# Norms moved into the other stream's stages, pieces spaced by declared costs, and a second set of value buffers in the first stage of a two-layer decoder kernel

## The reference, cut to what matters

```python
# D_MODEL 1024, SEQ 2048, layer 0: retention, 4 heads (dk 256, dv 512); layer 1: window attention, 16 heads of 64
for layer in range(2):
    hp, hs = rms_norm(xp, norm_mix[layer]), rms_norm(xs, norm_mix[layer])
    if layer == 0:    # chunks of 128; the state s is carried from chunk to chunk
        yp, sp = retention_mixer(hp, pos_p, 0, 128, w_q, w_k, w_v, w_g, w_o)
        ys, ss = retention_mixer(hs, pos_s, state_ret, 8, w_q, w_k, w_v, w_g, w_o)
    else:
        yp, kp, vp = swa_prompt(hp, ...); ys, kn, vn = swa_sample(hs, cache_k, cache_v, ...)
    xp, xs = xp + yp, xs + ys
    xp = xp + swiglu(rms_norm(xp, norm_ffn[layer]), w1, w3, w2)     # (silu(x@w1) * (x@w3)) @ w2, width 2816
    xs = xs + swiglu(rms_norm(xs, norm_ffn[layer]), w1, w3, w2)
y_prompt, y_sample = rms_norm(xp, norm_final), rms_norm(xs, norm_final)
# retention, one chunk of one head: o = (q k^T * decay) v + q s ; s = s*c + (k*kdecay)^T v ;
# then per row (o - mean) * rsqrt(var + eps), times silu(h @ w_g), then @ w_o
```

## Time and profile before

| | |
|---|---|
| Median of 3 runs | 2740.5 us (2739.23 to 2741.64) |
| Profiled execution, its own time | 2740.44 us |
| Its span on the slowest core (5) | 2739.4 us; the eight cores 2719.8 to 2739.4 |
| PE (matmul) busy | 2166.1 us, 79% |
| DVE, ACT, POOL busy | 1201.0, 771.6, 145.8 us |
| Mean granted TensorE clock, core 5 | 0.882 |
| HBM read and written | 332.78 and 104.60 MB |

### The profile page before, as it was taken

One profiled execution on the slowest core, in us unless ns is written; L12 is line 12 of the kernel. 1 busy time (PEld: TensorE's weight loads), 2 busy tenths in 40 slices (PEclk: granted clock), 3 DMA queues, 4 the chain that ended last, 5 costly groups with the idle time before them and its releaser, 6 DMA issues.

```text
span 2739.4 us, 39645 instructions; the slowest of 8 cores (2719.8 to 2739.4 us)
## 1 busy us (share of the span) xinstructions
PE 2166.1 (79%) x12058; PEld 1020.5 (37%) x12058; DVE 1201.0 (44%) x3034; ACT 771.6 (28%) x1480; POOL 145.8 (5%) x273
## 2 busy tenths in 40 slices
PE   3766588878688878868888688887879887867797
PEld 2322233333233334433333233333435444433454
DVE  3454345442345434543545444554244434543423
ACT  1323122231135223412323222323023422431211
POOL 0000001001000101100000010000000000000000
PEclk9877799988789989978999889988979998988898
DMA  8563667758665669763443464532413242211233
GB/s 198 127 161 76 167 173 173 178 156 182 159 183 169 187 172 220 174 190 127 157 149 134 139 198 160 176 113 73 147 62 105 70 116 76 83 55 58 92 114 104
DMA packets 136590, 380.34 MB, mean 139 GB/s; under 512 B 19744, under 2 KB 23968, under 8 KB 136352
## 3 DMA queue, kind: packets, MB, share of 16 engines
q1 hardware_dynamic: 103024, 282.36, 32.0%
q0 software_dynamic: 33360, 95.44, 17.4%
HBM read 332.78 MB, written 104.60 MB: 160 GB/s over the span
## 4 chain that ended last, share of the span: by engine, by line
PE 56%; DVE 18%; DMA 9%; issue 8%; ACT 6%; DVEq 1%; SPq 0%; ACTq 0%; POOL 0%; POOLq 0%
PE pb L434 55%; ACT arL L443 4%; DMA wbd<-wf 3%; DVE arL L449 2%; DVE arL L461 2%; PE pb L440 2%; DVE Sst L452 2%; DVE hT L452 2%; DMA arG<-st_in 1%; DMA wf<-wt 1%; DVE stat L455 1%; DVE stat L677 1%; DMA srs<-arG 1%; DVE stat L452 1%; ACT sq L443 1%
## 5 line engine op out<-in xcount | busy, mean ns | idle before, releaser
L434 PE MATMUL pb<-hT,wf 128*128 128x512 bf16 x2816 | 700.5, 404 | 16.7 <-DVE arF L452 5.6
L434 PEld LDWEIGHTS pb<-hT,wf 128*128 128x128 bf16 x2816 | 284.0, 103 | 381.9 <-issue 113.1
L434 PE MATMUL pb<-arF,wf 128*128 128x512 bf16 x1408 | 338.6, 391 | 4.4 <-DMA wf<-wt 4.1
L443 ACT ACTIVATE arL<-pb 128x512 bf16<-128x512 f32 (+2 forms) x278 | 200.0, 728 | 261.7 <-PE pb L434 219.0
L434 PE MATMUL pb<-wl,hT 128*128 128x512 bf16 (+1 forms) x1152 | 254.7, 374 | 5.3 <-DVE Sst L452 5.3
L452 DVE SCALAR_TENSOR_TENSOR arF<-arF,pb 128x512 f32<-128x512 f32 (+1 forms) x176 | 121.1, 688 | 299.5 <-ACT arF L443 229.3
L449 DVE TENSOR_TENSOR xT<-pb,xT 128x512 f32<-128x512 f32 x160 | 108.9, 690 | 317.0 <-PE pb L434 316.9
L434 PE MATMUL pb<-hT,wl 128*128 128x512 bf16 x800 | 217.7, 413 | 29.9 <-DVE hT L452 12.6
L440 PE MATMUL pb<-cbt,arL 128*128 128x128 bf16 x1056 | 97.8, 235 | 134.2 <-DVE arL L449 86.5
L434 PEld LDWEIGHTS pb<-arF,wf 128*128 128x128 bf16 x1408 | 138.0, 101 | 168.7 <-issue 29.0
L443 ACT ACTIVATE arF<-pb 128x512 f32<-128x512 f32 x176 | 105.8, 601 | 332.4 <-PE pb L434 326.5
(11 more groups left out here) (89 smaller groups left out, 2004.3 us busy)
## 6 DMA issues: line engine op xcount, KB each, us to landing
wl<-wbd SPq DMA_DIRECT2D x123, 512.0 KB, 5.0
wf<-wbd SPq DMA_DIRECT2D x120, 512.0 KB, 4.2
wf<-wbd SPq DMA_DIRECT2D x96, 352.0 KB, 3.2
arG<-st_in SPq DMA_DIRECT2D x128, 256.0 KB, 4.1
srs<-arG POOLq DMA_DIRECT2D x128, 256.0 KB, 3.5
wl<-wt POOLq DMA_DIRECT2D x41, 512.0 KB, 7.6
wbd<-wl SPq DMA_DIRECT2D x41, 512.0 KB, 10.0
wf<-wt POOLq DMA_DIRECT2D x40, 512.0 KB, 8.8
```

The costliest lines, as they stand in the source:

```text
L434: S.op("pe", lambda e: e.matmul(out, lhsT, rhs, start=start, stop=stop), r, w)
L443: S.op("act", lambda e: e.activation(out=out, in_=in_, func=func, bias=bias, scale=scale), r, w)
```

## The change

- `run`'s stages are paired anew. The norm that feeds a tile's next mixer now stands at the end of the feed-forward part of the stage before (`nm(0, 2, PF)` and its like, `swap`), and the norm that feeds a tile's feed-forward at the start of the feed-forward part, while part 0 starts at once with matmuls on an `hT` that is ready. In stage 8 the two norms for stage 9 stand at the end of part 0. The norm of tile 1 for stage 2 runs in stage 1 (`first_x1`).
- The `pc` numbers of `norm`, `scores` and `core` are raised; `norm` of a tile now counts 4 times 1300, then 4500, 2500 and 1500.
- `ffn` yields between the w1 and the w3 matmuls of a 512-column tile, and its first activation (for tanh also the VectorE instruction behind it) is recorded before the w3 matmuls, for the sample's 128 columns too.
- `layer0` of stage 1 (`deep`) has kd, v and g twice, the second set in `arF`, and lets out all of the next head's projections between its chunks; in the last head it lets out w_o matmuls of heads 0 to 2. `wo` adds into `xT` behind each 4 matmuls of the last head instead of at the end of a half.
- `gstream` loads its states on the POOL queue instead of SP's.
- The first loads stand in another order, and `load_x(1)` comes later. `swap` loads a later tile 10000 units of `pc` ahead of its norm.

```diff
@@ norm
-                    pc(60 * nch)
                     if kc % 2 == 1:
+                        pc(1300 if NT == TT else 700)
                         yield
...
                 rsq(n_[:, 0:nch], n_[:, 4:4 + nch], n_[:, 8:8 + nch], nb)
+                pc(4500)
                 yield
...
-                pc(500 * nch)
+                pc(2500)
                 yield
...
                     if after is not None:
                         after(kc)
+                pc(1500)
                 yield
@@ ffn
                                     b1, b3 = b1_[:, 0:NS], b3_[:, NS:2 * NS]
                                 else:
                                     b1, bb1, _ = pb(P)
-                                    b3, bb3, _ = pb(P)
+                                s1v = o.s1[:, s, :NT]
                                 for kc in range(KC):
                                     mm(b1[:, :NT], w1u[:, kc, fi * 128:(fi + 1) * 128], cx.hT[:, kc, :NT], kc == 0, kc == KC - 1,
                                        [w1b_, cx.hb[kc]], [bb1])
+                                if tanh:
+                                    act(s1v, b1[:, :NT], AF.Tanh, [bb1], [o.s1b[s]], scale=0.5)
+                                    stt(s1v, s1v, 1.0, b1[:, :NT], ALU.add, ALU.mult, [o.s1b[s], bb1], [o.s1b[s]])
+                                else:
+                                    act(s1v, b1[:, :NT], AF.Silu, [bb1], [o.s1b[s]])
+                                pc(8 * NT * 0.43)
+                                if NT > NS:
+                                    yield
+                                    b3, bb3, _ = pb(P)
                                 for kc in range(KC):
                                     mm(b3[:, :NT], w3u[:, kc, fi * 128:(fi + 1) * 128], cx.hT[:, kc, :NT], kc == 0, kc == KC - 1,
                                        [w3b_, cx.hb[kc]], [bb3])
-                                pc(16 * NT * 0.43)
-                                s1v = o.s1[:, s, :NT]
+                                pc(8 * NT * 0.43)
                                 if tanh:
-                                    act(s1v, b1[:, :NT], AF.Tanh, [bb1], [o.s1b[s]], scale=0.5)
-                                    stt(s1v, s1v, 1.0, b1[:, :NT], ALU.add, ALU.mult, [o.s1b[s], bb1], [o.s1b[s]])
                                     stt(o.aT[:, fl, :NT], s1v, 0.5, b3[:, :NT], ALU.mult, ALU.mult, [o.s1b[s], bb3], [o.ab[fl]])
                                 else:
-                                    act(s1v, b1[:, :NT], AF.Silu, [bb1], [o.s1b[s]])
                                     tt(o.aT[:, fl, :NT], s1v, b3[:, :NT], ALU.mult, [o.s1b[s], bb3], [o.ab[fl]])
                             if fi == nf - 1:
                                 RF.done(2)
@@ layer0
-            def layer0(cx, tile_i, P, rider=None, sfin=None):
+            def layer0(cx, tile_i, P, rider=None, sfin=None, deep=False):
...
+                if deep:
+                    AF_.reset()
+                kdA, vvA, ggA, kdbA, vbA, gbA = [], [], [], [], [], []
+                for A in ([AL, AF_] if deep else [AL]):
+                    kdA.append(A.alloc("kd", [128, nch, 256], BF16))
+                    vvA.append(A.alloc("v", [128, nch, 512], BF16))
+                    ggA.append(A.alloc("g", [128, nch, 512], BF16))
+                    kdbA.append([A.buf("kd") for _ in range(nch)])
+                    vbA.append([A.buf("v") for _ in range(nch)])
+                    gbA.append([A.buf("g") for _ in range(nch)])
+                nset = len(kdA)
...
+                def wo(half, hs):
+                    if hs[0] == 0:
+                        wob_[half] = [pb(P, True) for _ in range(4)]
+                    bs = wob_[half]
+                    if sfin is not None and half == 0 and hs[0] == 0:
+                        SF.c, SF.uTs, SF.uTsb = sfin()
+                    for h in hs:
...
+                            if h == RH - 1:
+                                kc = half * 4 + dm
+                                tt(cx.xT[:, kc, :NT], bs[dm][0][:, :NT], cx.xT[:, kc, :NT], ALU.add, [bs[dm][1], cx.xb[kc]], [cx.xb[kc]])
+                                P.free(bs[dm][2])
...
+                    if deep and nx:
+                        pieces = [p_qk(hd + 1, 0), p_qk(hd + 1, 1), p_vg(hd + 1, "v"), p_kd(hd + 1), p_vg(hd + 1, "g")]
+                    elif deep:
+                        pieces = [wo(0, list(range(RH - 1)))]
+                    else:
+                        pieces = [p_qk(hd + 1, 0), p_qk(hd + 1, 1)] if nx else []
+                    def step(n=1):
+                        while pieces and n:
+                            try:
+                                next(pieces[0])
+                                n -= 1
+                            except StopIteration:
+                                pieces.pop(0)
+                    scores(hd, 0)
+                    step(2 if deep else 1)
+                    pc(800)
+                    yield
+                    for c in range(nch):
+                        if c + 1 < nch:
+                            scores(hd, c + 1)
+                        core(hd, c)
+                        pc(1500)
+                        yield
+                        step(2 if deep else 1)
+                        if c > 0:
+                            tail(hd, c - 1)
+                        yield
+                        if deep:
+                            step(2 if nx else 1)
+                    while pieces:
+                        step()
+                        yield
...
+                if deep:
+                    yield from wo(0, [RH - 1])
+                else:
+                    yield from wo(0, list(range(RH)))
+                yield from wo(1, list(range(RH)))
@@ gstream
-                        dma("sp", S0[n % NR][:, :], st_in[b, h][a * 128:(a + 1) * 128, :], [], [S0b[n % NR]], f"g{n % NR}")
+                        dma("pool", S0[n % NR][:, :], st_in[b, h][a * 128:(a + 1) * 128, :], [], [S0b[n % NR]], f"g{n % NR}")
@@ body
...
+            def swap(t, P):
+                load_x(t)
+                pc(10000)
+                yield
+                yield from norm(pcx[t % 2], 0, P)
...
+            dma("pool", cb[:, 0:256], cb_d[:, 0:256], (), [cbb], "c1")
+            load_x(0)
+            RL.fill(2)
+            dma("sp", cf[:, :], cf_d[:, :], (), [cfb], "c2")
             dma("sp", sp[:, :], spar[:, :], (), [spb], "c0")
-            load_x(0)
-            dma("sp", cf[:, :], cf_d[:, :], (), [cfb], "c2")
-            dma("pool", cb[:, 0:256], cb_d[:, 0:256], (), [cbb], "c1")
-            RL.fill(3)
+            load_rope(0)
             dma("pool", cb[:, 256:CB_N], cb_d[:, 256:CB_N], (), [cbb2], "c3")
-            load_rope(0)
...
-            res[1] = run(1, [(lstage0(0, P1, rider=(s0c, rope_s)), 0, 1)])
+            def first_x1():
+                load_x(1)
+                pc(100)
+                yield
+                yield from norm(pcx[1], 0, P1)
+            res[1] = run(1, [(chain(norm(pcx[0], 0, P1), norm(s0c, 0, P1), layer0(pcx[0], 0, P1, (s0c, rope_s), None, True)), 0, 1), (first_x1(), 0.3, 0.85)])
             g = gstream()
             gall.append(g)
-            res[2] = run(2, [(lstage0(1, PL), 0, 1), (fstage(0, 0, False, PF), 0, 1)], 16, g)
+            res[2] = run(2, [(layer0(pcx[1], 1, PL), 0, 1), (chain(nm(0, 1, PF), ffnp(0, 0, False, PF), nm(0, 2, PF)), 0, 0.93)], 16, g)
             dma("sp", ks_o[:, 0:128 - DS, :], ck[:, DS:128, :], [], [], "ko")
             dma("sp", vs_o[:, 0:128 - DS, :], cv[:, DS:128, :], [], [], "ko")
-            res[3] = run(3, [(lstage1(0, PL), 0, 1), (fstage(1, 0, True, PF), 0, 1)], 40, g)
-            res[4] = run(4, [(lstage1(1, PL), 0, 1), (fstage(0, 1, True, PF), 0, 0.9)], 8, g)
-            res[5] = run(5, [(lstage0(2, PL), 0.12, 1), (fstage(1, 1, False, PF), 0, 0.92)], 38, g)
-            res[6] = run(6, [(lstage0(3, PL, sf=sfin), 0.12, 1), (fstage(2, 0, False, PF), 0, 1)], 26, g, 0.55)
-            res[7] = run(7, [(lstage1(2, PL), 0, 1), (fstage(3, 0, True, PF4, True), 0, 1)])
-            res[8] = run(8, [(lstage1(3, PL, True), 0, 1), (fstage(2, 1, True, PF), 0, 1)])
-            res[9] = run(9, [(fstage(3, 1, False, P1, True), 0, 1)])
+            res[3] = run(3, [(layer1(pcx[0], 0, PL), 0, 1), (chain(nm(1, 1, PF), ffnp(1, 0, True, PF), nm(1, 2, PF)), 0, 0.93)], 40, g)
+            res[4] = run(4, [(layer1(pcx[1], 1, PL), 0, 1), (chain(nm(0, 3, PF), ffnp(0, 1, True, PF), fin(0, PF), swap(2, PF)), 0, 0.95)], 8, g)
+            res[5] = run(5, [(layer0(pcx[0], 2, PL), 0, 1), (chain(nm(1, 3, PF), ffnp(1, 1, False, PF), fin(1, PF), swap(3, PF)), 0, 0.95)], 38, g)
+            res[6] = run(6, [(layer0(pcx[1], 3, PL, None, sfin), 0, 1), (chain(nm(2, 1, PF), ffnp(2, 0, False, PF), nm(2, 2, PF)), 0, 0.93)], 26, g, 0.55)
+            res[7] = run(7, [(layer1(pcx[0], 2, PL), 0, 1), (chain(nm(3, 1, PF4), snorm(1, PF4), ffnp(3, 0, True, PF4, True), nm(3, 2, PF4), snorm(2, PF4)), 0, 0.95)])
```

(2 more changed lines are left out.)

104 lines of the change are left out of this document (34 added, 70 removed).

## The result

| | before | after |
|---|---|---|
| Median | 2740.5 us | 2611.4 us |
| Ratio, 95% interval | | 0.952 (0.949 to 0.955) |
| Span of the profiled execution, slowest core | 2739.4 us | 2610.4 us (core 1) |
| PE busy | 2166.1 us | 2105.2 us |
| PE idle in the span | 573 us | 505 us |

The change gains 129 us; 2480 was forecast, with a range up to 2600.

A forecast was written before the change was run, and what follows sets the result against it. PE, idle 573 us of 2739.4, was held by uncovered dependent norm and chunk chains. Idle terms -109 - 59 - 24 - 23 + 46 = -169 us, plus 92 us of slow matmuls saved, gave about 2480 us, range 2395 to 2600.

The forecast's parts named there:

- Norms beside the other stream: -109 us of waits: Norms in all stages: new neighbours cover their chains, removing 109 us of PE waits, bounds 60 and 150.
- The chunk chain: `layer0` in stages 2, 5 and 6: new `pc` numbers put matmuls behind each group, -59 us of idle time.
- stage 1's buffers: Stage 1 (`deep`): projections fill the gaps of three heads of four, -24 us of idle time, bounds 0 and -45.
- the state stream: Stages 3, 7, 8 and `gstream`: finer pieces meet half of the waits, -23 us, between 0 and 47.
- The shared bank: Sample's feed-forward, stages 7 and 9: PE waits for the bank's readers, 22 times each, +46 us of idle time.
- State loads on POOL: State loads issued from POOL, two units ahead: 0 us by themselves.
- The state loads turn the time round: Rival, chance 0.05: POOL's queue delays state casts, mainly stages 2 and 4; slower, 2863 us at 3 us each.
- its own sign: Sign against the forecast: ACT waiting for `arG<-st_in` more than before.
- The conversion of idle time into time: Whole kernel: each microsecond of long PE wait removed also saves 0.43 us of slow matmuls, 92 us in all.
- Covers work half: Rival, chance 0.17: DVE and ACT queues hold chains up, half of the 215 us goes, 2632 us.
- the 215 us: Long PE waits forecast to go over the whole kernel: 169 us of idle time plus the bank's 46.
- Weights bind: Rival, chance 0.06: weight transfers limit stages 1 to 4, which gain nothing, 2630 us.

The follow-up runs named there:

- e6: The kernel after with every norm and load of x back in its old stage and part, all else kept; ratio 0.9711, 2661 us.
- f2: The kernel after with tile 1's norm moved among the w_o matmuls at the end of stage 1, its loads issued before the stage; 2569 us.
- e7: The kernel after with `deep` set to False, so one set of value buffers in stage 1; ratio 0.9577, 2625 us.
- e3: The kernel after with the sample's first activation recorded behind both products again; ratio 0.9280, 2543 us.
- e4: The kernel after with the retention state loads issued from SP's queue again instead of POOL's; ratio 0.9478, 2597 us.
- f3: The kernel after with the edits of e3 and f2, and the norms' squares recorded one piece ahead of their sums except in stage 8; 2482 us.

## Why the prediction was wrong

**The step that failed is "Norms beside the other stream: -109 us of waits".** The 204.7 us became 187.9, or 198 with the 10.2 for `smpd`, which had counted as `sq`: 7 gone instead of 96. That is 89 of the 101 us by which the idle time (505 instead of 404) was missed; the other 31 us by which the span was missed are PE's busy time (2105 instead of 2074). By e6 not even the 7 come from the placement: with the norms in their old place, and all numbers new, they wait less. I read the order of PE and asked how many matmuls stand ahead of a piece ("about 5 each" in seven paired stages). I did not ask what stands ahead of the squares on ScalarE. Stages 2 and 6 have 2 us each for `sq`; their norms stand among w_o or feed-forward matmuls, as I read it with nothing late ahead. Stages 3, 4 and 5 have 66 us for `sq` against the 28 of my sum (5 each and 13 for the swaps), and stages 7 and 8 have 25 for `sq` and `nst` against 10. In stage 3 that is the cast of the earlier trace rows, for which I had counted the state loads on POOL as freeing it. The norm of tile 1, new in stage 1, I gave no wait at all; it has 29 us there, and stage 1 is 39 us longer by it (e6, f2). The first norms have 47 instead of 33 us (8.8 of them are the kernel's first wait, which before was put down to `cb`), the last 13 as forecast; the start of stage 2 waits 10.2 us for `smpd` (14 forecast). The 11.8 us in stage 4 (10 forecast) are the swap's: there ScalarE waits for tile 2 itself, as the sum had it.

**The chunk chain, stage 1's buffers, the state stream: right in the sum, less so by stage.** The waits for `arL` fell by 92 us: by 32 in stage 1 (from 59.2, with 2.6 us that the earlier trace rows leave out, to 27.4; -28 forecast), by 44 in stages 2, 5 and 6 (110.9 to 66.5; -59 forecast), and by 16 in the others (a part of the 23). But the sum took them as separate from the norms' term, and e6 shows that they are not: with the norms back in their old place these waits are 45 us longer. What e7 takes back is 15 us of time.

**The shared bank: mechanism right, price too small.** In e3 51 us of idle time go, against 46 forecast, but I gave these waits no clock: 66 us of time. "1.05 to 2.0" in stage 7 measured 1.92 each.

**State loads on POOL: 0 forecast, perhaps 12 lost.** If the 12 us of e4 are real, the rival *The state loads turn the time round* has the right sign and a price far too high; its own sign, ACT waiting longer for `arG<-st_in`, did not show (158.3 us before, 104.2 after).

**The conversion of idle time into time: the agreement is in part luck.** The forecast turned 404 us of idle time into a span of 2478, and f3 has 401 us and 2480.7. But the 404 held 46 us of bank waits at no price in clock, and f3 has none of these. From before to f3 172 us of idle time went; at 0.43 they would have taken 74 us of busy time with them, and they took 86 (2166.1 to 2080.1), 0.50 for each. In after 61 us of busy time went; with the 20 that the bank's waits cost (e3), that is 81 for the 119 us of other waits that went (68 + 51), 0.68 for each. So 0.43 was too low in both, and the free bank waits were too cheap; the two errors work against each other.

**The rivals.** *Covers work half* gave 2632, and 119 of the 215 us went. But it is not half everywhere, as it said; stages 2, 6, 7, 8 and 9 came out as forecast, and with three edits of order (f3) the time is 2482. *Weights bind* gave 2630, as near, by another way: it had stages 1 to 4 gain nothing, and stage 2 gained 46 us at a DMA share of 0.83. In stage 4 it has a small part: there `wf` from `wt` is 14.4 us of PE's waits (8.6 before) at a share of 0.82.

## What to carry to other kernels

Before an instruction is placed beside work that covers it, read the queue of the engine that makes its input: what is late ahead of it there is what the consumer waits for, however much stands ahead of the consumer itself. Record a producer one piece before its consumer and keep both away from instructions that wait for a load or for a long chain on another engine. Declared latencies and placement are one change: test them as a two by two table before either is credited, and look at which waits change, since a moved norm can shorten its neighbour's waits and not its own.
